# Moving the normed activations by 1472 bytes against the split weights in a two-block transformer kernel

## The reference

```python
h = rms_norm(x, norm_mix_pre);  u = h @ w_in                 # 2048 x 4352
y = concat(mixers(u)) @ w_out;  x = x + rms_norm(y, ...)      # 2048 x 2048
h = rms_norm(x, norm_ffn_pre);  up = h @ w_up                 # 2048 x 11264
x = x + rms_norm((silu(gate) * val) @ w_down, ...)            # 5632 x 2048
# second block: w_in_2 (2048 x 11272), w_branch_m, w_branch_a (1024 x 2048 each),
# w_out_2 (2048 x 2048), w_up_2 (2048 x 8192), w_down_2 (8192 x 2048)
```

## Time and profile before

| | |
|---|---|
| median of 3 runs | 2491.93 us (2491.35 to 2492.01) |
| profiled execution, first to last instruction | 2489.1 us |
| TensorE busy | 2471.2 us, 99% of the span, 15394 matmuls |
| TensorE weight loads busy | 2211.0 us, 89% |
| VectorE busy | 1745.7 us, 70% |
| ScalarE busy | 1278.2 us, 51% |
| HBM read | 455.15 MB, 184 GB/s over the span |
| granted TensorE clock | 1.00 of full in all but a few microseconds |

### The profile page before, as it was taken

The page is one execution under the profiler, slowest core; times in us unless marked ns, Lnnn a source line. Parts: engine busy times, 40 slices in busy tenths (PEclk is TensorE's granted clock), DMA queues, the critical chain, the costliest instruction groups (busy, mean ns, idle before and its releaser), DMA issues.

```text
span 2489.1 us, 38802 instructions
## 1 busy us (share of the span) xinstructions
PE 2471.2 (99%) x15394; PEld 2211.0 (89%) x15394; DVE 1745.7 (70%) x2277; ACT 1278.2 (51%) x1627; POOL 36.9 (1%) x35
## 2 busy tenths in 40 slices
PE   9999999999999999999999999999999999999999
PEld 9999998888888888888888888899888888888887
DVE  8998597765876577797777766664875565665665
ACT  6345565544554455666654444445544444444454
POOL 0000100000000000100000000001000000000001
PEclk9999999999999999999999999999999999999999
DMA  8565546555565555555655566655565655655652
GB/s 285 164 195 170 186 159 196 186 188 191 179 202 186 186 186 186 178 170 178 186 170 176 172 189 190 187 186 191 165 203 186 186 187 190 190 193 186 186 187 102
DMA packets 308053, 459.10 MB, mean 184 GB/s; under 512 B 14790, under 2 KB 156371, under 8 KB 307923
## 3 DMA queue, kind: packets, MB, share of 16 engines
q1 hardware_dynamic: 304112, 456.34, 57.5%
q10 hardware_dynamic: 3810, 0.94, 0.2%
HBM read 455.15 MB, written 2.11 MB: 184 GB/s over the span
## 4 chain that ended last, share of the span: by engine, by line
PE 96%; DVE 2%; ACT 1%; issue 1%; DMA 0%; SPq 0%; DVEq 0%; ACTq 0%
PE ps L691 26%; PE ps L689 23%; PE ps L692 13%; PE ps L688 11%; PE ps L697 5%; PE ps L698 5%; PE ps L699 5%; PE ps L793 1%; PE ps L791 1%; PE ps L733 1%; PE ps L737 1%; PE ps L734 1%; PE ps L794 1%; DVE w_split L1761 1%; PE ps L790 1%
## 5 line engine op out<-in xcount | busy, mean ns | idle before, releaser
L1761 DVE TENSOR_TENSOR w_split<-raw,w_split 128x1024 fp32r<-128x1024 f32 (+1 forms) x856 | 1044.9, 1223 | 692.5 <-ACT w_split L1133 690.0
L1133 ACT ACTIVATE w_split<-raw 128x1024 fp32r<-128x1024 f32 x853 | 901.0, 1059 | 1014.7 <-PE ps L689 806.4
L691 PE MATMUL ps<-h_split,w_split 128*128 128x512 f32 x1802 | 706.0, 397 | 0.1
L689 PE MATMUL ps<-h_split,w_split 128*128 128x512 f32 x1590 | 629.2, 396 | 0.0
L692 PE MATMUL ps<-h_split,w_split 128*128 128x256 f32 x1802 | 500.6, 278 | 0.0
L688 PE MATMUL ps<-h_split,w_split 128*128 128x256 f32 x1590 | 443.2, 279 | 0.0
L692 PEld LDWEIGHTS ps<-h_split,w_split 128*128 128x128 f32 x1802 | 339.0, 188 | 67.8
L691 PE MATMUL ps<-act_split,w_split 128*128 128x512 f32 x1004 | 390.8, 395 | 0.4 <-DVE scaled L1761 0.3
L688 PEld LDWEIGHTS ps<-h_split,w_split 128*128 128x128 f32 x1590 | 298.5, 188 | 72.3
L691 PEld LDWEIGHTS ps<-h_split,w_split 128*128 128x128 f32 x1802 | 341.7, 190 | 11.1 <-DVE w_split L1761 1.1
L689 PE MATMUL ps<-act_split,w_split 128*128 128x512 f32 x868 | 343.6, 396 | 0.0
(11 more groups left out here) (301 smaller groups left out, 2959.7 us busy)
## 6 DMA issues: line engine op xcount, KB each, us to landing
raw<-w_up SPq DMA_DIRECT2D x152, 1024.0 KB, 5.2
raw<-w_in SPq DMA_DIRECT2D x114, 1024.0 KB, 5.3
raw<-w_down SPq DMA_DIRECT2D x108, 1024.0 KB, 5.1
raw<-w_out SPq DMA_DIRECT2D x32, 1024.0 KB, 5.1
raw<-w_in SPq DMA_DIRECT2D x16, 512.0 KB, 4.9
raw<-w_branch_m SPq DMA_DIRECT2D x8, 1024.0 KB, 5.7
raw<-w_branch_a SPq DMA_DIRECT2D x8, 1024.0 KB, 5.7
outT<-x SPq DMA_DIRECT2D x7, 256.0 KB, 2.1
```

Of the source, the lines that this page charges most:

```text
L689: last = nc.tensor.matmul(wide, hi[:, cols], rhs[:, k, :], start=False, stop=end)
L691: nc.tensor.matmul(wide, hi[:, cols], rhs[:, k, :], start=first, stop=False)
L1133: nc.scalar.activation(split_home(n)[0], raw[:, slot, half:half + 1024], ACT.Copy).then_inc(hi_ready, 1)
L1761: return nc.vector.tensor_tensor(out, a, b, op)
```

## The change

An unused region of 1472 bytes is taken ahead of `h_split`. `h_split`, `act_split` and all that `place` and `region` give out behind them, region C and `merged` among it, move up by 1472 bytes. `raw`, `w_split` and `x` stay. No instruction is added, removed or reordered. Of the pairs of weights and activations, `w_split` with `h_split` and `w_split` with `act_split` go from a distance of 0 to one of 1472 modulo 2048; `w_split` with `merged` goes from 1472 to 2944, which is 896 modulo 2048; the early homes keep their distance to `h_split`, since both move.

```diff
         w_split = place("w_split", [128, SPLIT_SLOTS, 2, 1024], f32r)
         w_hi, w_lo = w_split[:, :, 0, :], w_split[:, :, 1, :]
         x = place("x", [128, KT, T])
+        STAGGER = 1472
+        region(STAGGER)
         h_split = place("h_split", [128, KT, 2 * T], f32r)
         ACT_SPLIT = top[0]
         act_split = place("act_split", [128, KT, 2 * T], f32r)
```

## The result

| | before | changed |
|---|---|---|
| median of the runs | 2491.97 us (2491.35 to 2492.78) | 2478.27 us (2477.98 to 2481.22) |
| profiled execution | 2489.1 us | 2476.2 us |
| ratio, 95% interval | | 0.9949 (0.9937 to 0.9961) |

The change makes the kernel 0.5% faster, 13.7 us. Forecast were 2431 us, 60.7 us less. The sign is right, the size is off by more than four times. The time lies outside the forecast's own range, 2405 to 2456, and beside that of the rival "triples only", 2477.5 us, in the part (2457 to 2486) that had a chance of 0.18.

A forecast was written before the change was run, and what follows sets the result against it. TensorE's matmul stream, 99% busy, was taken as the bound. Terms -17.6 - 2.6 - 46.3 + 2.5 + 3.3 = -60.7 us turn the profiled 2489.1 into 2428.4, median 2431 us; own range 2405 to 2456, 8 in 10 within 2402 to 2492.

The forecast's parts named there:

- triples only: Rival: the pairs don't respond to the residue, only the triple streams gain; 2477.5 us, chance 0.18 (including a few ns of pairs).
- TensorE's stream is the bound: Whole kernel: TensorE is 99% busy with 96% of the last-ending chain, so only closer matmul starts can shorten it.
- It is the residue and not the region: Opposed the rival that region C makes streams fast and moving buffers changes nothing: 2491.9 us, chance 0.10.
- both fast cases: Matmuls on `merged` and from the early home in C, both in region C, far behind `w_split` and `h_split`.
- Term (a): Triples on `h_split` and `act_split`: 2640 matmuls at 6.7 ns, 17.6 us less; openings from `w_split`, 2.6 us less.
- Term (b): 5264 pairs of 512- and 256-row matmuls: from 348.9 to 340.1 ns each, 46.3 us less; bounds 70.5 less, 24.2 more.
- The sign that the prediction saw in the stream itself: In the pairs, 512-row matmuls are followed after 0.23 or 0.24 us by weight-tile place, taken as response to residue.
- Term (c): 768 matmuls on `merged`, moved to 896 modulo 2048 off the weights: 2.5 us more, bounds 0 and 5.1.
- Term (d): First mixer, 120 to 200 us: nearly full VectorE limits the gain to 1.2 of 4.5 us, so 3.3 us are lost.
- The rule of the Trainium skill: TensorE's reads: it never waits on anyone and has two independent read ports, so no address matters; time stays 2492 us.
- Slower: Rival: a new collision in the 5264 pairs, weight loads against streamed reads; up to 2504.3 us, deciding from 2.7 ns a pair; chance 0.15.

The follow-up runs named there:

- merged_back: The changed kernel with 576 more free bytes ahead of region C, so `merged` has its old residue against `w_split`; 2479.08 us, ratio 0.9947 to the kernel before.

## Why the prediction was right and wrong, step by step

**TensorE's stream is the bound, and only the distance of starts can change.** Right in the main: the instructions are the same, and the time went where the intervals did, less what new waits and the clock took back (below).

**It is the residue and not the region.** Right, shown by the shift of 2048. The chance of 0.10 for the rival was fair; its argument was good, since both fast cases did lie in one region.

**Term (a), the triples, -20.2 us.** The price is right for `h_split` (113.5 against a forecast of 113.3), and its stage gave 10.7 us. On `act_split` it was 116.3, because most of the stream is in the second state: 1104 x (119.9 - 116.3) gives 4.0 us where 6.7 ns each would be 7.4. The openings from `w_split` fell from 119.9 to 115.1 ns, 384 x 4.8 = 1.8 us where 2.6 were forecast. The prediction had both prices of that state in hand, said that one distance needn't give one value, and didn't carry it into the sum.

**Term (b), the pairs, -46.3 us. This step failed.** It measured 5264 x (348.8 - 347.3) = 7.9 us, and of the 47 us between forecast and result 38 are here. The step took the lowest price that a 256-row and a 512-row matmul show anywhere and gave it to all of them, as if each had a price of its own at a good residue. The runs show in its place a price that belongs to the sequence: the same low-then-high order costs 340.0 ns inside the alternation and 353.1 by itself; a gain in one of the four matmuls comes with a loss in another; and halves placed apart don't add. Eight residues, five placements with the halves apart and five cases of a like order gave 345.5 to 355.5 ns. The row that should have warned was one the prediction read the other way: the gate matmuls took 226.8 ns at the "bad" residue 0, where the 512-row matmuls of the pairs took 233. Residue alone could not be what parts them, so a good residue could not be expected to close that gap. The gate matmuls rise to 232.8 in the mean at the residue of the change. And 226.8 is the price of the settled end of their stream before; the first five of the 16 took 229 to 236 ns. No row showed a pair at another residue, and the 46.3 rested on single prices taken from other streams. The sign that the prediction saw in the stream itself, 0.23 and 0.24 us in turn behind a 512-row matmul, was no sign of residue either: the two places differ by 1024 bytes, which is 0 modulo 256, and after the change both are followed after 0.236 us.

**Term (c), merged, +2.5 us.** Measured 3.9 to 4.0 us (768 x 5.2 ns); inside its bounds.

**Term (d), what is late next, +3.3 us.** The engine is right, VectorE in the mixer; the place and the wait are not. Between 120 and 200 us TensorE has 704 matmuls where it had 663, with no idle time, while VectorE is busy 79.86 of 80 us:

```profile
120.00:200.00 80.00, 80.00 (x704) 79.90 (x703) 79.86 (x142) 33.94 (x37) 0.00 (x0) 1.00 0.60 188
```

That is 41 x 0.12 = 4.9 us gained where the prediction allowed 1.2, and no wait for low halves. The bill came behind the stage. From 197.7 to 323.0 us the stretch is 125.3 us long, and was 123.1 before, though its triples and openings are some 4 us cheaper: about 6 us more. Of these 3.9 us are idle time (waits of 4.5 us against 0.6), and 1.3 are 13 more starts at the lower level of the clock. The row with VectorE's busy share told how full it was but not which of its work would be called in late, and where.

**The sum.** The terms as measured, 10.0 + 4.0 + 1.8 for the triples, 7.9 for the pairs, less 4.0 for `merged`, make 19.7 us; the span is shorter by 12.9. Between them stand the 3.9 us of new idle time and, in this one pair of traces, 27 more starts at the lower level of the clock, 213 to 214 ns apart (41 against 14), 27 x 0.098 = 2.6 us. Two of the three places where the clock is low in the changed kernel lie behind waits that the kernel before has as well, so how much of this belongs to the change isn't shown.

**The rule of the Trainium skill.** The Trainium skill, SBUF — State Buffer, section "SBUF: two separate sides", would have TensorE wait for no one, and the Trainium skill, TensorE: Matmul & The Clock Gate, under the drain step, gives it two independent read ports. The shift of 2048 against that of 1472, and the move of the low weights alone, disagree with what would follow from that: 120.0 against 113.5 ns for the same instructions. What can't be told is where the two reads meet.

**The rivals.** "Triples only" named the time (2477.5) with the right main reason, that the disturbance in the pairs isn't the steady one of the triples. That it meets the time to a microsecond is luck: the pairs do respond and gave 7.9 us that it puts at nothing, the triples gave 4.4 less than it counts, `merged` took 1.5 more, and waits and the clock took more than its 3.3. "Slower" is true of the neighbours: at 96 a pair costs 4.1 ns more than at 0, beyond the 2.7 from which the prediction said that it decides, and that kernel is slower.

**Open.** Why the period is 256 bytes, what fixes which state a triple stream takes, and whether any order and placement reach 340. In the traces of the changed kernel and of merged_back the states change only where other matmuls or a gap interrupt the stream; nothing was run that sets them.

## What to carry to other kernels

Where a matmul stream is the bound, compare start distances of the same instruction on different tensors; a difference of some ns is a hint that the buffers' residues matter, and a few kernels with other padding, each carrying two or three residues, are a cheap search. Don't price a mixed stream from the best values of its parts: only what the whole sequence showed can be expected, and a lone price is a bound. When a stage that feeds on another engine gets faster, look past its end for the place where that engine's lag is called in.

## What the runs showed of the hardware that was not expected

- Matmuls that read fp32r activations while the next weights load start 113.3 to 120.0 ns apart in a stream of 256 rows. In a mixed stream they take 113.6 to 123 ns for 256 rows and 226 to 237 for 512. It depends on the distance modulo 256 bytes between the two addresses within a partition, and on the order of the matmuls.
- At residues 192 and 64 the triple stream has two steady prices, 113.3 and 117.8 ns, and passes from one to the other where it is interrupted, by a gap or by a few other matmuls.
- At the lower level of the clock the surcharge of the triples is gone. In the kernel before TensorE waits 2.1 us for ScalarE up to 307.0 us, and from 308.2 on the granted clock is 0.50 of full, 1.2 GHz. These two starts lie 6 matmuls apart, 0.2133 us each, which is 256 rows at 1.2 GHz and nothing more, while at full clock the lowest price, 113.3 ns, is 6.6 ns above 256 rows at 2.4 GHz:

```profile
308.81 0.41 PE L734 MATMUL ps<-h_split,early_lo 128*128 128x256 f32 x1
...
310.09 0.41 PE L734 MATMUL ps<-h_split,early_lo 128*128 128x256 f32 x1
...
308.80:310.10 1.30, 1.30 (x8) 1.30 (x8) 1.30 (x4) 0.96 (x3) 0.00 (x0) 0.50 0.03 6
```

The home lies at a distance of 64 modulo 256 there. The changed kernel has 213 to 214 ns at the lower level at distances of 192, 64 and 0.
